# Retention chunks taken two by two between runs of sixteen projection matmuls

## The chip, the cores and the metric

The kernel runs on one core of a Trainium2 chip, as one program. The metric is the device time of one execution in microseconds (us); the median of several executions is compared. The engines that matter here are TensorE (PE: matmuls; its weight loads are listed apart, as PEld), VectorE (DVE) and ScalarE (ACT). Each works through its own instruction list in order, and they wait for one another on semaphores.

## What is computed

Four layers over 1024 tokens of width 1024: a dilated attention layer, a state space layer, and then two "hybrid" layers. Only the retention branch of the hybrid layers is touched. It has 6 heads of 64 channels and works in chunks of 128 tokens, forward and backward in time:

```python
def chunk_retention(q, k, v, lg, s0, inclusive):
    ...
    scores = jnp.einsum('bhnid,bhnjd->bhnij', qc, kc) * dmat[None, :, None]
    o_inner = jnp.einsum('bhnij,bhnje->bhnie', scores, vc)
    ...
    _, s_prev = lax.scan(step, s0, jnp.moveaxis(u, 2, 0))
    ...
    o_cross = jnp.einsum('bhnid,hi,bhnde->bhnie', qc, wq, s_prev)
    return (o_inner + o_cross).reshape(b, h, l, dv)

def bidir_retention(q, k, v, lg_f, lg_b, s_f, s_b):
    fwd = chunk_retention(q, k, v, lg_f, s_f, True)
    bwd = chunk_retention(jnp.flip(q, 2), jnp.flip(k, 2), jnp.flip(v, 2), lg_b, s_b, False)
    return fwd + jnp.flip(bwd, 2)
```

So a chunk needs scores (queries times keys), their product with a decay matrix, the inner output (masked scores times values) and the cross output (queries times the state before the chunk), and both outputs are added. Around it stand the input projections `h @ w_in`, which are by far the larger work.

## The kernel before

Everything is unrolled. A hybrid layer `l` (0 or 1) does its projections in groups `j`, and while PE does the projections of group `hp + 1` it also does the retention of head pair `hp` (0 to 2), whose q, k, v and gate came from group `hp`. In `mix_pe`, `ret_segment(hp)` writes PE's order down by hand: `proj(j, x0, x1)` issues the projection matmuls x0 to x1 of the group, and the retention matmuls are put between such runs at fixed positions (`RET_A` to `RET_F`). 24 projection matmuls make a part; a part is 512 or 256 tokens wide, fills PSUM bank 0 or 1 in turn, and is evacuated by ACT (`evac`), after which that bank may be used again (`g_evac`). A projection matmul is in fp32r, 128 rows by 128 columns of the array.

The chunks: `chunks(l)` is 10 in layer 0 (8 of the sequence, 2 of the context) and 8 in layer 1, so there are 3 x 10 + 3 x 8 = 54. Of one chunk `n` PE issues

- `inner(n)`, the scores: 2 matmuls, one per head, each on 64 rows and 128 columns of the array, into banks 5 and 6 (even n) or 2 and 3 (odd n). It needs those banks read, that is the masked scores of chunk n - 2 (`r_sd`), and for n = 1 the scan of the states (`r_scan`);
- the cross product: 4 matmuls (2 directions x 2 heads) on 64 rows and 64 columns, into bank 7 (even n) or 4 (odd n), once ACT has copied chunk n - 2 out of it (`r_o`);
- the inner output: 2 matmuls on 128 rows and 64 columns, added to the same bank, once DVE has made the masked scores `SD[:, n % 2]` (`r_sd`). The last one releases `r_omul`.

All of these are fp32, and the trace has two MATMUL records for each. DVE makes `SD` of chunk n (L1929) when the scores are there (`r_s`) and, as it has two buffers, when the output of chunk n - 2 is done (`r_omul`). ACT copies the finished chunk to `RO` (L1741) when `r_omul` of that chunk is there, and the evacuations of projection parts stand between these copies on its list. After the last chunk come 10 more projection matmuls and then the matmul that takes the mean (L1554), which waits for all copies.

The constants: `RET_D` = 102 is where `inner(0)` stands, `RET_O` = 112 where the outputs begin, `RET_STEP` = 8. In the loop of before, `proj` runs up to matmul 112 + 8n, then come `inner(n + 1)` and `out_of(n)`, where `out_of` is the cross product and the inner output together.

One other place is spoken of further on: in the state space layer `outputs_of` (L3032, L3041) and `turn_natural` (L822) follow each other on PE, and each begins with a wait (`pe.wait_ge(s_loaded[...], ...)`, `pe.wait_ge(y_gelu, ...)`), though both are work of 128 rows and 128 columns.

Of the kernel before, what the change touches and what calls it, by code (L numbers as in the profile page):

```python
# [133 lines left out]
def build(nc, io, out):  # L134
    x_in = io["x"].rearrange("b s d -> (b s) d")
    ctx = ExitStack()
    with ctx:
# [1167 lines left out]
        def parts_before(l, j):  # L1305
            return sum(len(PARTS[a][b]) for a in range(2) for b in range(N_GROUPS) if (a, b) < (l, j))
# [13 lines left out]
        def n_mms(l, j):  # L1320
            return 24 * len(PARTS[l][j])

        def chunks(l):
            return NC if l == 0 else NT
# [8 lines left out]
        RET_A, RET_B, RET_C, RET_D, RET_O, RET_STEP = 12, 48, 74, 102, 112, 8  # L1333
# [115 lines left out]
        def mix_pe(pe, l, early=None):  # L1449

            def proj(j, x0, x1):

                parts = PARTS[l][j]
                for x in range(x0, min(x1, n_mms(l, j))):
                    i, m = x // 24, x % 24
                    q, c0, c, last = parts[i]
                    n, slot = parts_before(l, j) + i, slot_of(l, j, q)
                    k = m // 3
                    w, a = PASSES[m % 3]
                    if m == 0:  # L1460
                        if j == 0 and q == 0:
                            pe.wait_ge(t_lo, rows_there(l, c0))
                        pe.wait_ge(g_evac[n % 2], EVACS_DONE + n // 2)
                        if c0 == 0:
                            pe.wait_ge(slot_split, slot + 3)
                    ins = nc.tensor.matmul(psum[:, n % 2, 0:c], w[:, slot % 2, k * P:(k + 1) * P], a[:, k, c0:c0 + c],  # L1466
                                           start=(m == 0), stop=(m == 23))
                    if m == 23:
                        ins.then_inc(slot_used if last else half_done, 1)
# [12 lines left out]
            def ret_segment(hp):  # L1482
                j, it = hp + 1, hp + 3 * l
                tk, tv, tq, tg = SETS[hp % 2]
                base = chunk_base(l, hp)

                def inner(n):
                    if n == 1:
                        pe.wait_ge(r_scan, it + 1)
                    if n >= 2:  # L1490
                        pe.wait_ge(r_sd, base + n - 1)
                    for h in range(2):
                        ins = nc.tensor.matmul(psum[:, inner_banks(n)[h], 0:P], tk[HALF[h], n * P:(n + 1) * P],  # L1493
                                               tq[HALF[h], n * P:(n + 1) * P], start=True, stop=True)
                    ins.then_inc(r_s, 1)

                def out_of(n):
                    if n >= 2:
                        pe.wait_ge(r_o, base + n - 1)
                    o = psum[:, cross_bank(n), 0:P]  # L1500
                    for d, v in enumerate((tv, TMP)):
                        for h in range(2):
                            nc.tensor.matmul(o[HALF[h]], SFC[HALF[h], d, n], v[HALF[h], n * P:(n + 1) * P],  # L1503
                                             start=(d == 0), stop=False, skip_group_check=True)
                    pe.wait_ge(r_sd, base + n + 1)
                    for h in range(2):
                        ins = nc.tensor.matmul(psum[HALF[h], cross_bank(n), 0:P], VR[:, n, 64 * h:64 * h + 64],  # L1507
                                               SD[:, n % 2, h * P:(h + 1) * P], start=False, stop=True, skip_group_check=True)
                    ins.then_inc(r_omul, 1)

                proj(j, 0, RET_A)
                group_there(hp)
                if hp == 0:
                    pe.wait_ge(p_const, 16 * 2 * (l + 1))
                if hp > 0:
                    pe.wait_ge(r_eps, it)
                for i, t in enumerate((tk, tq)):
                    for c in range(2):
                        ins = nc.tensor.matmul(psum[:, 2 + 2 * i + c, :], C_PERM, t[:, c * 512:(c + 1) * 512], start=True, stop=True)  # L1519
                    ins.then_inc(r_swap, 1)  # L1520
                for n in range(8):
                    ins = nc.tensor.transpose(psum[:, 6 + n // 4, (n % 4) * P:(n % 4 + 1) * P], tv[:, n * P:(n + 1) * P], ident[:, :])
                    if n % 4 == 3:
                        ins.then_inc(r_vt, 1)
                proj(j, RET_A, RET_B)
                pe.wait_ge(r_rope, 2 * it + 2)
                for n in (8, 9):
                    ins = nc.tensor.transpose(psum[:, 5, (n - 8) * P:(n - 7) * P], tv[:, n * P:(n + 1) * P], ident[:, :])
                ins.then_inc(r_vt, 1)
                for n in range(NC):  # L1530
                    ins = nc.tensor.transpose(psum[:, 2 + n // 4, (n % 4) * P:(n % 4 + 1) * P], tk[:, n * P:(n + 1) * P], ident[:, :])
                ins.then_inc(r_kt, 1)
                proj(j, RET_B, RET_C)
                pe.wait_ge(r_rows, it + 1)
                pe.wait_ge(r_vr, 3 * it + 3)
                for d, w in enumerate((KF, KBW)):
                    for n in range(NC):
                        for h in range(2):
                            ins = nc.tensor.matmul(state_tile(d, n)[HALF[h]], w[:, n, 64 * h:64 * h + 64],  # L1539
                                                   VR[:, n, 64 * h:64 * h + 64], start=True, stop=True)  # L1540
                ins.then_inc(r_u, 1)
                proj(j, RET_C, RET_D)
                inner(0)
                at = RET_D
                for n in range(chunks(l)):
                    proj(j, at, RET_O + RET_STEP * n)
                    at = RET_O + RET_STEP * n
                    if n + 1 < chunks(l):
                        inner(n + 1)
                    out_of(n)  # L1550
                proj(j, at, RET_E[l])
                pe.wait_ge(r_o, base + chunks(l))
                for i, (c0, c) in enumerate(segs_of(l, False)):
                    ins = nc.tensor.matmul(psum[:, 5 + i, 0:c], C_ONES, RO[:, c0:c0 + c], start=True, stop=True)  # L1554
                ins.then_inc(r_mean, 1)
                proj(j, RET_E[l], RET_F[l])
                pe.wait_ge(r_sq, it + 1)
                for i, (c0, c) in enumerate(segs_of(l, False)):
                    ins = nc.tensor.matmul(psum[:, 2 + i, 0:c], C_ONES, TMP[:, c0:c0 + c], start=True, stop=True)
                ins.then_inc(r_var, 1)  # L1560
                proj(j, RET_F[l], n_mms(l, j))
# [76 lines left out]
            for hp in range(3):  # L1638
                ret_segment(hp)
# [3 lines left out]
        def mix_act(act, l, early=False):  # L1643
# [81 lines left out]
            def ret_segment(hp):  # L1725
                j, it = hp + 1, hp + 3 * l
                base = chunk_base(l, hp)
                evacs(j, 0, RET_A)
                for i in range(2):
                    act.wait_ge(r_vt, 3 * it + i + 1)  # L1730
                    C.copy(VR[:, 4 * i:4 * i + 4].rearrange("p n c -> p (n c)"), psum[:, 6 + i, :]).then_inc(r_vr, 1)
                evacs(j, RET_A, RET_B)
                act.wait_ge(r_vt, 3 * it + 3)
                C.copy(VR[:, 8:10].rearrange("p n c -> p (n c)"), psum[:, 5, 0:256]).then_inc(r_vr, 1)
                evacs(j, RET_B, RET_O)
                at = RET_O
                for n in range(chunks(l)):
                    evacs(j, at, RET_O + RET_STEP * n)
                    at = RET_O + RET_STEP * n
                    act.wait_ge(r_omul, base + n + 1)  # L1740
                    C.copy(RO[:, n * P:(n + 1) * P], psum[:, cross_bank(n), 0:P]).then_inc(r_o, 1)  # L1741
                evacs(j, at, RET_E[l])
                if hp < 2:
                    decays(hp + 1)
                w = P * chunks(l)
                act.wait_ge(r_cent, it + 1)
                C.activation(TMP[:, 0:w], RO[:, 0:w], ACT.Square).then_inc(r_sq, 1)
                evacs(j, RET_E[l], RET_F[l])
                act.wait_ge(r_eps, it + 1)
                C.activation(TMP[:, 0:w], TMP[:, 0:w], ACT.Sqrt).then_inc(r_root, 1)  # L1750
                evacs(j, RET_F[l], n_mms(l, j))
# [2102 lines left out]
```

## Time and profile before

| | |
|---|---|
| median of 3 runs | 3284.87 us (3284.24 to 3288.15) |
| profiled execution, its own time | 3281.52 us |
| its span, first to last instruction | 3279.7 us |
| PE busy | 3218.2 us, 98% of the span |
| DVE, ACT, POOL busy | 1409.6, 1242.2, 805.1 us |
| mean granted TensorE clock | 0.998 |
| chunk operations on PE | 54 chunks in 60 places between projection runs |

A row of the timeline gives the start, the time from there to the end of the last instruction of the group, the engine, the line of the kernel and what it does; "64*128" is rows by columns of the array that are used. Matmuls overlap: the time of one is longer than its distance to the next, so the distance between two starts is what an instruction costs PE. The profile's rows are in the section "Rows read from the trace of the kernel before".

### The profile page before, as it was taken

The page shows a single profiled execution, that of the slowest core. Times are in us where ns is not written, and L with a number is a line of the kernel's source. Part 1 is how long each engine was busy: PE and PEld are TensorE (multiplying, and loading weights), DVE is VectorE, ACT ScalarE, POOL GpSimd, SP SyncE. Part 2 cuts the span into 40 slices and gives each one's busy share as a digit, 9 for nine tenths or more (in the row PEclk, how much of TensorE's full clock was granted, in tenths as well). Part 3 has the DMA queues.
Part 4 walks back from the last instruction along what each step waited for, and adds up shares of the span by engine and source line. Part 5 has one row for each costly group of instructions (what it writes and reads, how often), then busy time and mean ns, then how long its engine had stood idle before and what let it go on. Part 6 is the DMA issues. An engine that isn't in the chain of part 4 may idle for free.

```text
span 3279.7 us, 49108 instructions
## 1 busy us (share of the span) xinstructions
PE 3218.2 (98%) x19729; PEld 2572.3 (78%) x19729; DVE 1409.6 (43%) x3279; ACT 1242.2 (38%) x2570; POOL 805.1 (25%) x407
## 2 busy tenths in 40 slices
PE   8999999999999999999999999999999999999999
PEld 6777877788787777778888877777788777777787
DVE  3343223221212137498234344345446724464566
ACT  4443444433443444321323322255333413255342
POOL 2155454111111132324343111101222111110231
PEclk9999999999999999999999999999999999999999
DMA  7122323244434234213534200101104310111113
GB/s 191 44 61 77 84 59 84 66 121 143 110 91 114 79 103 133 93 58 131 206 110 136 65 26 27 33 26 31 30 23 154 98 34 26 31 40 31 33 43 137
DMA packets 311271, 260.99 MB, mean 80 GB/s; under 512 B 61829, under 2 KB 275161, under 8 KB 311050
## 3 DMA queue, kind: packets, MB, share of 16 engines
q10 hardware_dynamic: 115152, 130.49, 13.3%
q1 hardware_dynamic: 195898, 127.41, 13.2%
q8 instruction: 157, 2.57, 0.3%
q14 instruction: 64, 0.52, 0.1%
HBM read 220.87 MB, written 48.58 MB: 82 GB/s over the span
## 4 chain that ended last, share of the span: by engine, by line
PE 53%; DVE 4%; ACT 2%; issue 1%; DMA 1%; ACTq 1%; POOL 0%; DVEq 0%; POOLq 0%
PE psum L1466 24%; PE psum L379 9%; PE psum L301 5%; PE psum L1578 2%; PE psum L1598 2%; PE psum L1587 2%; PE psum L1503 1%; PE psum L3041 1%; DVE act_lo L2472 1%; PE psum L1493 1%; PE psum L1519 1%; PE psum L1507 1%; DVE arena L1908 1%; PE psum L3032 1%; PE psum L1539 0%
## 5 line engine op out<-in xcount | busy, mean ns | idle before, releaser
L2644 POOL TENSOR_TENSOR w_lo<-w_raw,w_hi 128x1024 fp32r<-128x1024 f32 x122 | 294.9, 2417 | 1539.4 <-ACT w_hi L1701 773.2
L1466 PE MATMUL psum<-act_hi,w_hi 128*128 128x512 f32 (+1 forms) x1376 | 513.0, 373 | 4.6 <-ACT arena L1687 2.1
L2814 PE MATMUL psum<-act_hi,w_hi 128*128 128x512 f32 x1280 | 505.4, 395 | 4.7 <-ACT arena L1187 3.6
L2814 PE MATMUL psum<-act_lo,w_hi 128*128 128x512 f32 x1280 | 507.1, 396 | 0.0
L1466 PE MATMUL psum<-act_lo,w_hi 128*128 128x512 f32 (+1 forms) x1376 | 506.8, 368 | 0.0
L1466 PE MATMUL psum<-act_hi,w_lo 128*128 128x512 f32 (+1 forms) x1376 | 505.7, 367 | 0.0
L2814 PE MATMUL psum<-act_hi,w_lo 128*128 128x512 f32 x1280 | 503.4, 393 | 0.0
L3595 DVE CUSTOM_DVE_ANT_0 arena<-psum,arena 128x128 f32<-128x128 f32 (+1 forms) x384 | 112.1, 348 | 480.2 <-PE psum L2853 333.2
L1466 PEld LDWEIGHTS psum<-act_hi,w_hi 128*128 128x128 f32 x1376 | 259.8, 189 | 59.1 <-issue 16.1
L1466 PEld LDWEIGHTS psum<-act_hi,w_lo 128*128 128x128 f32 x1376 | 259.5, 189 | 46.9 <-issue 7.0
L1466 PEld LDWEIGHTS psum<-act_lo,w_hi 128*128 128x128 f32 x1376 | 260.1, 189 | 45.1 <-issue 9.0
L2814 PEld LDWEIGHTS psum<-act_hi,w_hi 128*128 128x128 f32 x1280 | 240.6, 188 | 62.5 <-issue 7.3
L2814 PEld LDWEIGHTS psum<-act_lo,w_hi 128*128 128x128 f32 x1280 | 240.7, 188 | 59.9 <-issue 11.7
L2814 PEld LDWEIGHTS psum<-act_hi,w_lo 128*128 128x128 f32 x1280 | 240.6, 188 | 54.8 <-issue 5.9
L2635 POOL TENSOR_TENSOR w_hi<-w_raw,one 128x1024 fp32r<-128x1024 f32 x48 | 95.1, 1982 | 679.7 <-PE psum L1466 294.7
L1187 ACT ACTIVATE arena<-psum 128x512 f32<-128x512 f32 x144 | 133.0, 923 | 185.6 <-PE psum L2814 155.6
L3131 ACT ACTIVATE arena<-arena 128x128 f32<-128x128 f32 (+1 forms) x384 | 168.5, 441 | 76.6 <-DVE arena L3595 75.9
L3179 ACT COPY arena<-psum 128x1024 f32<-128x1024 f32 (+1 forms) x96 | 83.7, 872 | 269.8 <-PE psum L2871 218.7
L1779 ACT COPY arena<-psum 128x896 f32<-128x896 f32 (+1 forms) x108 | 91.5, 848 | 159.3 <-PE psum L1598 118.2
L2638 POOL TENSOR_TENSOR w_lo<-w_raw,w_hi 128x1024 fp32r<-128x1024 f32 x48 | 125.4, 2613 | 3.8
L1770 ACT ACTIVATE arena<-arena 128x512 f32<-128x512 f32 (+1 forms) x96 | 72.3, 753 | 122.0 <-DVE arena L2003 122.0
L301 PE MATMUL psum<-w_hi,act_hi 128*128 128x512 f32 x256 | 100.2, 391 | 5.8 <-DVE act_lo L452 3.1
(397 smaller groups left out, 5428.6 us busy)
## 6 DMA issues: line engine op xcount, KB each, us to landing
w_raw<-in_attn_w_in SPq DMA_DIRECT2D x80, 512.0 KB, 3.7
w_raw<-in_w_in SPq DMA_DIRECT2D x64, 512.0 KB, 4.0
spare<-in_w_mod ACTq DMA_DIRECT2D x24, 1024.0 KB, 7.9
x<-arena ACTq DMA_DIRECT2D x24, 512.0 KB, 2.9
arena<-weight_rows ACTq DMA_DIRECT2D x16, 512.0 KB, 6.7
w_raw<-in_ssm_w_in SPq DMA_DIRECT2D x16, 512.0 KB, 3.8
arena<-mc_mat ACTq DMA_DIRECT2D x16, 512.0 KB, 3.7
arena<-x ACTq DMA_DIRECT2D x16, 512.0 KB, 5.3
```

The lines of the kernel that those rows point to most:

```text
L301: ins = nc.tensor.matmul(psum[:, t, :], a[:, k, t * P:(t + 1) * P], w[:, par, i * 512:(i + 1) * 512], start=(k == 0 and a is act_hi and w ...
L379: ins = nc.tensor.matmul(psum[:, bank + c, :], a[:, k, t * P:(t + 1) * P], w[:, c * 512:(c + 1) * 512], start=(i == 0 and w is hi and a is ...
L1187: return nc.scalar.activation(dst, src, ACT.Copy, scale=SCALE if p % 3 == 0 else 1.0)
L1466: ins = nc.tensor.matmul(psum[:, n % 2, 0:c], w[:, slot % 2, k * P:(k + 1) * P], a[:, k, c0:c0 + c], start=(m == 0), stop=(m == 23))
L1779: C.copy(PT2[h][:, c0:N_LOG], flat(6, 2)[:, c0:N_LOG]).then_inc(u_pt, 1)
L2635: G.tensor_tensor(w_hi[:, par], w_raw[:, par], one[:, 0:1].to_broadcast([P, 1024]), ALU.mult).then_inc(slot_hi, 1)
L2638: G.tensor_tensor(w_lo[:, par], w_raw[:, par], w_hi[:, par].bitcast(F32), ALU.subtract).then_inc(slot_split, 1)
L2644: G.tensor_tensor(w_lo[:, par], w_raw[:, par], w_hi[:, par].bitcast(F32), ALU.subtract).then_inc(slot_split, 1)
L2814: ins = nc.tensor.matmul(psum[:, h % 2, :], w[:, (3 + j) % 2, k * P:(k + 1) * P], a[:, k, c:c + 512], start=(m == 0), stop=(m == 23))
L3131: nc.scalar.activation(lg, lg, ACT.Exp, scale=-1.0, bias=st[:, 2 + h, u:u + 1], accum_out=st[:, h, u:u + 1]).then_inc(u_probs, 1)
L3179: nc.scalar.copy(PT.rearrange("p a (h c) -> p a h c", h=2)[:, :, :, 0:c], psum[:, 4:6, :].rearrange("p a (h c) -> p a h c", h=2)[:, :, :, ...
L3595: nc.vector.tensor_tensor_reduce(LOG[:, a, h * 256:h * 256 + P * nk], psum[:, 2 + h, 256 * a:256 * a + P * nk], BIAS[:, h, bias_cols(g, u) ...
```

## The change

The cross product becomes a function of its own, `cross(n)`. The chunks are taken in pairs: after a run of projection matmuls come the scores of chunks n + 2 and n + 3, the cross products of n and n + 1, and then the inner outputs of n and n + 1. The runs between pairs are 16 matmuls instead of 8. `inner(1)` stands alone at position 112, and the first pair comes at 120. On ACT the copies of both chunks of a pair stand at the pair's position in its list. DVE's list is the same. Positions of all later work (`RET_E`, `RET_F`) are unchanged.

```diff
@@ -1494,7 +1494,7 @@
-                def out_of(n):
+                def cross(n):
                     if n >= 2:
                         pe.wait_ge(r_o, base + n - 1)
                     o = psum[:, cross_bank(n), 0:P]
@@ -1502,6 +1502,8 @@
                         for h in range(2):
                             nc.tensor.matmul(o[HALF[h]], SFC[HALF[h], d, n], v[HALF[h], n * P:(n + 1) * P],
                                              start=(d == 0), stop=False, skip_group_check=True)
+
+                def out_of(n):
                     pe.wait_ge(r_sd, base + n + 1)
                     for h in range(2):
                         ins = nc.tensor.matmul(psum[HALF[h], cross_bank(n), 0:P], VR[:, n, 64 * h:64 * h + 64],
@@ -1541,13 +1543,19 @@
                 inner(0)
-                at = RET_D
-                for n in range(chunks(l)):
-                    proj(j, at, RET_O + RET_STEP * n)
-                    at = RET_O + RET_STEP * n
-                    if n + 1 < chunks(l):
-                        inner(n + 1)
+                proj(j, RET_D, RET_O)
+                inner(1)
+                at = RET_O
+                for n in range(0, chunks(l), 2):
+                    proj(j, at, RET_O + RET_STEP * (n + 1))
+                    at = RET_O + RET_STEP * (n + 1)
+                    if n + 2 < chunks(l):
+                        inner(n + 2)
+                        inner(n + 3)
+                    cross(n)
+                    cross(n + 1)
                     out_of(n)
+                    out_of(n + 1)
                 proj(j, at, RET_E[l])
@@ -1735,8 +1743,8 @@
                 for n in range(chunks(l)):
-                    evacs(j, at, RET_O + RET_STEP * n)
-                    at = RET_O + RET_STEP * n
+                    evacs(j, at, RET_O + RET_STEP * (n // 2 * 2 + 1))
+                    at = RET_O + RET_STEP * (n // 2 * 2 + 1)
                     act.wait_ge(r_omul, base + n + 1)
                     C.copy(RO[:, n * P:(n + 1) * P], psum[:, cross_bank(n), 0:P]).then_inc(r_o, 1)
```

PE's list, layer 0, first head pair, before: the places of chunks 1 and 2, with the run of 8 projection matmuls between them cut. In these rows 128x128 and 64x128 are the shapes of the output. L1493 are scores, L1503 cross products, L1507 inner outputs.

```order
L1493 MATMUL psum<-arena 128x128 [waits r_sd]
L1493 MATMUL psum<-arena 128x128
L1503 MATMUL psum<-arena 64x128 x4
L1507 MATMUL psum<-arena 64x128 [waits r_sd]
L1507 MATMUL psum<-arena 64x128
L1466 MATMUL psum<-act_hi,w_hi 128x256 [waits g_evac1]
...
L1493 MATMUL psum<-arena 128x128 [waits r_sd]
L1493 MATMUL psum<-arena 128x128
L1503 MATMUL psum<-arena 64x128 [waits r_o]
L1503 MATMUL psum<-arena 64x128 x3
L1507 MATMUL psum<-arena 64x128 [waits r_sd]
L1507 MATMUL psum<-arena 64x128
```

The same place now: the pair of chunks 2 and 3 (scores of 4 and 5), where L1509 are the inner outputs.

```order
L1493 MATMUL psum<-arena 128x128 [waits r_sd]
L1493 MATMUL psum<-arena 128x128
L1493 MATMUL psum<-arena 128x128 [waits r_sd]
L1493 MATMUL psum<-arena 128x128
L1503 MATMUL psum<-arena 64x128 [waits r_o]
L1503 MATMUL psum<-arena 64x128 x3
L1503 MATMUL psum<-arena 64x128 [waits r_o]
L1503 MATMUL psum<-arena 64x128 x3
L1509 MATMUL psum<-arena 64x128 [waits r_sd]
L1509 MATMUL psum<-arena 64x128
L1509 MATMUL psum<-arena 64x128 [waits r_sd]
L1509 MATMUL psum<-arena 64x128
```

Operations of one kind and one shape of the array now stand in a row for two chunks, and the second of each kind has a wait in the middle of that row.

ACT's list, the same layer and head pair, before (L1689 evacuates a projection part, L1701 rounds weights, L1741 copies a chunk):

```order
L1689 COPY arena<-psum 128x512 [waits half_done]
L1741 COPY arena<-psum 128x128 [waits r_omul]
L1689 COPY arena<-psum 128x512 [waits half_done]
L1741 COPY arena<-psum 128x128 [waits r_omul] x3
L1689 COPY arena<-psum 128x256 [waits slot_used]
L1701 CAST w_hi<-w_raw 128x1024 [waits slot_hi,slot_loaded1]
L1741 COPY arena<-psum 128x128 [waits r_omul] x3
```

And now (L1697, L1709 and L1749 are the same three):

```order
L1697 COPY arena<-psum 128x512 [waits half_done] x2
L1749 COPY arena<-psum 128x128 [waits r_omul] x4
L1697 COPY arena<-psum 128x256 [waits slot_used]
L1709 CAST w_hi<-w_raw 128x1024 [waits slot_hi,slot_loaded1]
L1749 COPY arena<-psum 128x128 [waits r_omul] x2
```

The copies moved behind the evacuation of the part that ends at the first pair, and the later ones come two by two.

## Rows read from the trace of the kernel before

**Rows 1.** The page: busy time of the engines, and the chain by engine.

```profile
PE 3218.2 (98%) x19729; PEld 2572.3 (78%) x19729; DVE 1409.6 (43%) x3279; ACT 1242.2 (38%) x2570; POOL 805.1 (25%) x407
...
PE 53%; DVE 4%; ACT 2%; issue 1%; DMA 1%; ACTq 1%; POOL 0%; DVEq 0%; POOLq 0%
```

**Rows 2.** Windows: one head pair, layer 0: PE, PEld, DVE, ACT, POOL busy; clock.

```profile
1860.00:1944.00 84.00, 83.91 (x570) 64.36 (x569) 35.07 (x52) 22.24 (x43) 9.82 (x4) 1.00 0.09 26
```

**Rows 3.** Waits of weight loads, 1800 to 3182 us: total us, times, longest.

```profile
PEld psum L1493 <- issue: 15.9, 45, 0.4
...
PEld psum L1507 <- DVE arena L1929: 8.3, 48, 0.2
```

**Rows 4.** Timeline of PE: one place of before, between 512-wide projection matmuls.

```profile
1892.41 0.39 PE L1466 MATMUL psum<-act_hi,w_hi 128*128 128x512 f32 x1
1892.73 0.49 PE L1493 MATMUL psum<-arena 64*128 64x128 f32 x4
1893.15 0.65 PE L1503 MATMUL psum<-arena 64*64 64x128 f32 x8
1893.74 0.44 PE L1507 MATMUL psum<-arena 128*64 128x128 f32 x4
1894.11 0.50 PE L1466 MATMUL psum<-act_lo,w_hi 128*128 128x512 f32 x1
1894.44 0.39 PE L1466 MATMUL psum<-act_hi,w_lo 128*128 128x512 f32 x1
1894.67 0.40 PE L1466 MATMUL psum<-act_hi,w_hi 128*128 128x512 f32 x1
```

**Rows 5.** Timeline of PE: another place, between 256-wide projection matmuls.

```profile
1898.34 0.28 PE L1466 MATMUL psum<-act_hi,w_hi 128*128 128x256 f32 x1
1898.46 0.28 PE L1466 MATMUL psum<-act_lo,w_hi 128*128 128x256 f32 x1
1898.67 0.49 PE L1493 MATMUL psum<-arena 64*128 64x128 f32 x4
```

**Rows 6.** One line: DVE's masked scores, all 54 (duration min/median/max).

```profile
L1929 DVE TENSOR_TENSOR arena<-psum,arena x54: 424/425/426, 1890.4 to 2853.8; 128x256 f32<-128x256 f32 x54
```

**Rows 7.** Timeline of PE in the attention layer: four matmuls on 64*128 in a row.

```profile
70.97 0.72 PE L2827 MATMUL psum<-arena 64*128 64x128 f32 x8
71.61 0.50 PE L2814 MATMUL psum<-act_hi,w_hi 128*128 128x512 f32 x1
```

**Rows 8.** Timeline of PE in the neighbourhood attention: twelve matmuls on 128*64 in a row.

```profile
2154.45 1.53 PE L1598 MATMUL psum<-arena 128*64 128x128 f32 x24
2155.91 0.70 PE L1578 MATMUL psum<-arena 64*128 64x512 f32 x2
```

**Rows 9.** Timeline of PE in the state space layer: groups of equal shape, each behind a wait.

```profile
1580.19 0.60 PE L822 MATMUL psum<-ident,arena 128*128 128x128 f32 x4
1580.63 0.61 PE L3032 MATMUL psum<-arena 128*128 128x128 f32 x4
```

**Rows 10.** Timeline of DVE: masked scores of the chunk whose scores stand in rows 4.

```profile
1893.27 0.42 DVE L1929 TENSOR_TENSOR arena<-psum,arena 128x256 f32<-128x256 f32 x1 [2.49 <-PE psum L1493]
```

**Rows 11.** Timeline of ACT: copy of the chunk of rows 4, and a later part.

```profile
1894.22 0.27 ACT L1741 COPY arena<-psum 128x128 f32<-128x128 f32 x1 [5.07 <-PE psum L1507]
...
1903.80 0.37 ACT L1689 COPY arena<-psum 128x256 f32<-128x256 f32 x1 [0.87 <-PE psum L1466]
1904.07 1.05 ACT L1701 CAST w_hi<-w_raw 128x1024 fp32r<-128x1024 f32 x1
```

**Rows 12.** Timeline of PE: the end of the last chunk of layer 1, to the mean.

```profile
2857.68 0.38 PE L1466 MATMUL psum<-act_hi,w_hi 128*128 128x256 f32 x1
...
2858.97 0.59 PE L1554 MATMUL psum<-arena 128*128 128x512 f32 x1
```

**Rows 13.** Timeline of ACT there: the part before that chunk, and the chunk's copy.

```profile
2856.83 0.59 ACT L1693 COPY arena<-psum 128x512 f32<-128x512 f32 x1 [1.76 <-PE psum L1466]
2857.79 0.27 ACT L1741 COPY arena<-psum 128x128 f32<-128x128 f32 x1 [0.38 <-PE psum L1507]
```

## Prediction

> **What bounds the kernel now.** I read the page first. PE is busy 98% of the span, and the chain that ended last is mostly PE, while DVE, ACT and POOL are busy 43, 38 and 25% [rows 1]. Then the windows: in the 84 us around the retention of one head pair PE is busy 83.91 us at a granted clock of 1.00 (2.4 GHz), while DVE has 35 and ACT 22 us of work [rows 2]. Whatever shortens PE's list there shortens the program, as long as nothing else gets late.
>
> Next, what PE does in those 84 us. A busy row does not say that PE works at its peak, so I read starts. The waits list puts 8.3 us in 48 pieces of at most 0.2 us on "DVE L1929", and 15.9 us in 45 pieces of at most 0.4 us on "issue" [rows 3]. Neither is a true wait: DVE had finished the masked scores of that chunk a step earlier, and pieces of one size at each change of line look like a fixed price. The timeline shows it [rows 4]. Projection matmuls start 0.23 us apart (1894.44 to 1894.67). Around a chunk the starts are 1892.41 (last projection), 1892.73 (scores), 1893.15 (cross), 1893.74 (inner output), 1894.11 and 1894.44 (projections). From this a place costs:
>
> - entry: 1892.73 - 1892.41 - 0.23 = 0.09
> - scores I (4 records): 1893.15 - 1892.73 = 0.42
> - cross X (8 records): 1893.74 - 1893.15 = 0.59
> - inner output O (4 records): 1894.11 - 1893.74 = 0.37
> - exit: 1894.44 - 1894.11 - 0.23 = 0.10
>
> Together 1.57 us. Between 256-wide matmuls, 0.12 apart, the entry is the same: 1898.67 - 1898.46 - 0.12 = 0.09 [rows 5].
>
> Each kind uses another shape of the array (128*128, 64*128, 64*64, 128*64). How much of I, X and O is the price of changing shape and how much is streaming follows from longer runs of one shape. Four matmuls on 64*128 (8 records) take 71.61 - 70.97 = 0.64 us to the next shape [rows 7], where two take 0.42 [rows 4]. Twelve matmuls on 128*64 (24 records) take 2155.91 - 2154.45 = 1.46 us [rows 8], where two (4 records) take 0.37 [rows 4]: the other 20 records cost 1.09, or 0.055 each.
>
> **The change, part by part.** It removes no matmul and adds none. It changes how often PE changes shape.
>
> *Places.* Before, one head pair had `inner(0)`, and then one place per chunk: 11 in layer 0 and 9 in layer 1, times three, 60. Now there are `inner(0)`, `inner(1)` and one place for two chunks: 7 and 6, times three, 39. So 21 entries and exits go: 21 x 0.19 = 4.0 us.
>
> *Scores.* Two chunks' scores stand in a row 4 times per head pair in layer 0 and 3 times in layer 1, 21 in all. Two single I cost 0.84, a double one 0.64 [rows 4, 7]: 21 x 0.20 = 4.2 us.
>
> *Inner outputs.* Doubled 5 and 4 times, 27 in all. The second adds 4 x 0.055 = 0.22 instead of 0.37: 27 x 0.15 = 4.05 us.
>
> *Cross products.* Doubled 27 times. No row shows a longer run on 64*64. The bounds are that nothing is saved (the second costs 0.59 again) and that as much is saved as in the scores (0.20). I take 0.055 for each of the 8 records of the second, the pace of the 128*64 run, which moves the same 128 columns per record and has two matmuls side by side too: 0.44 instead of 0.59, 27 x 0.15 = 4.05 us (0 to 5.4).
>
> The sum is 4.0 + 4.2 + 4.05 + 4.05 = 16.3 us (12.3 to 17.7 by the bounds of the cross product).
>
> *The added waits inside a row* (the second scores, the second cross product, the second inner output: 21 + 21 + 27 = 69) I cost at nothing, if the semaphore is there in time. In the state space layer the group of L3032 also has a wait of its own and has the same shape as that of L822 ahead of it: 1580.63 - 1580.19 = 0.44 for 4 records, 0.11 each, no break [rows 9].
>
> *Are they in time?* DVE first, the cover that changes most. It makes `SD` of chunk n + 2 when the output of n is done. Before, that was past when the scores arrived, so DVE began 0.12 after them (1893.15, 1893.27), with a whole run in hand [rows 4, 10]. Now both products of a pair begin only when `out_of(n)` and `out_of(n + 1)` are done, at the end of the place. Two products of 0.425 us [rows 6] and some 0.12 us of signal for each make about 1.1 us, and the next scores, which wait for the first of them, come after 16 projections: 16 x 0.12 = 1.9 us in the one run that is 256 wide throughout, up to 16 x 0.23 = 3.7 in the others. Slack 0.8 us and more. The first pair's `inner(3)` waits for `SD` of chunk 1, whose scores stand 8 wide projections, 1.8 us, ahead, and the product ends 0.12 + 0.42 = 0.54 us after the scores: in time. Nothing else is queued on DVE there but the next head pair's decays, behind the last product, which now come 8 projections earlier.
>
> ACT: copies of 0.27 us, now two after each place, needed by the cross products 16 projections later. Between them stand evacuations (0.59 or 0.37 us) and a rounding of weights (1.05 us) [rows 11, 13]. Where a part ends just at a place, this work begins with the place, and a double place lasts 0.64 + 1.03 + 0.59 = 2.3 us, so ACT is free (0.59 + 1.05 = 1.6 us) when the place ends. At the end of a layer 1 pair the mean comes 1.29 us after the place (2857.68 to 2858.97) [rows 12]; the last copy now starts when the one before it ends, some 0.1 us later than before, when it ended 0.38 us after the place (2857.79 + 0.27 = 2858.06) [rows 13]. Slack 0.8 us. POOL and SP have the same lists, and their weights are needed at the same positions, 3 us in 84 earlier, with POOL busy 10 us of 84 [rows 2].
>
> *A rule against it.* In the run of rows 8 the matmuls of one pair and the next use the same rows of the array, and a pair of records costs 0.11 us, no more than the streaming, so their weight loads lie under the matmuls in flight. The Trainium skill, "TensorE: Matmul & The Clock Gate", part 3 (packing small matmuls), states that a weight load overlaps matmuls in flight only when its row group differs; by that rule the loads in the doubled rows would stay exposed, which is rival 2 below. Rows 8 speak against it.
>
> The profiled execution took 3281.52 us for a span of 3279.7, and the median is 3284.87, 3.3 us more; I take the gain off the median: 3284.87 - 16.3 = **3268.6 us** (a profiled execution at about 3265).
>
> **The rivals.**
>
> 1. *A wait in a row costs as much as a change of shape.* Then 21 double scores, 21 double cross products and 27 double outputs save nothing: 4.2 + 3.15 + 4.05 = 11.4 us less gain, 4.9 us left, 3280.0 us. For it: the waiting loads in the list are all at changes of shape, so this pattern is not in the retention. Against: rows 9. Chance 3%.
>
> 2. *Weight loads of the second chunk stay exposed.* A first load shows in the starts as 0.42 - 2 x 0.11 - 0.10 (the entry's size, for draining) = 0.10 us on 128 columns, and 0.37 - 2 x 0.11 - 0.10 = 0.05 on 64 [rows 4]. The second scores have two such steps (0.20), the second cross four (0.20), the second output two (0.10). The savings become 0, -0.05 and 0.05: 0 - 1.35 + 1.35 + 4.0 = 4.0 us, 3280.9 us. Against: rows 7 and 8. Chance 3%.
>
> 3. *Slower: the products of DVE get late.* They are tied to the end of a place, and PE waits for them at the next. The point from which it costs anything is a chain of 1.9 us (3.7 in wide runs) against my 1.1. To end slower by 6.6 us it must eat 16.3 + 6.6 = 22.9 us in the 21 places that begin with scores, 1.1 us each, so a chain of some 4.8 us in wide runs. For it: it is the one dependence that really became tighter. Against: 54 products of 424 to 426 ns without exception [rows 6]. Chance 2% for slower; 4% for a few places that wait, 3270 to 3277 us.
>
> 4. *The order doesn't reach the hardware.* It does: the list has the rows two by two. What may still go is the gain after it, if a later stage waits for something that does not follow PE. The chain has 1% of DMA [rows 1]; 3% that over 9.7 us is lost there and the result is within 0.2%.
>
> **How the numbers follow.** Forecast 85%, rivals 3, 3, 2 (and 4 for its mild form) and 3. The forecast's own range is 12.3 to 17.7 us of gain, 3267 to 3273, and the runs of before spread from 0.6 below to 3.3 above their median. I take 3264 to 3276: it holds the forecast and most of the mild form. A measurement of this kernel can tell about 0.2%, 6.6 us, from no change, so faster is below 3278.3: 85 + 4 + 1 = 90%; rivals 1, 2 and most of 4 are the same: 8%; slower 2%.
>
> **What would show it.** In the profile of the changed kernel, a full place should have its scores (8 records) 0.64 us ahead of the cross products, these (16 records) 1.03 us ahead of the inner outputs, and these (8 records) 0.59 us ahead of the projection; entry 0.09 and exit 0.10. 2.45 us stand for two places of 1.57. The "L1929" wait should fall from 48 pieces to one per place, 27 (24 with scores, fewer where it is named otherwise), still at most 0.2 us. If the cross takes 1.18, the upper bound was right; if the second of a kind starts 0.1 us late, rival 1 or 2, told apart by whether it is at the waiting record alone or at every pair. A longer idle row with L1929 behind it ahead of L1493 is rival 3. What would make the forecast wrong with all of this right is a wait on DMA or POOL that grew elsewhere by 10 us.

## The result

| | before | after |
|---|---|---|
| median | 3286.36 us (5 runs, 3284.24 to 3288.15) | 3268.76 us (5 runs, 3263.08 to 3275.58) |
| ratio after / before | | 0.9948, 95% interval 0.9935 to 0.9962 |
| profiled execution, span | 3279.7 us, clock 0.998 | 3273.8 us, clock 0.993 |
| places on PE | 60, 86.0 us | 39, 69.7 us |

The forecast was 3268.6 us. Five more executions of the changed kernel, taken later, gave 3268.93 (first experiment below).

The page of the changed kernel, the same rows as [rows 1]:

```profile
PE 3211.9 (98%) x19729; PEld 2579.8 (79%) x19729; DVE 1405.6 (43%) x3279; ACT 1241.6 (38%) x2570; POOL 800.1 (24%) x407
...
PE 53%; DVE 4%; ACT 2%; issue 1%; DMA 1%; ACTq 1%; POOL 0%; DVEq 0%; POOLq 0%
```

PE has the same number of records and is still the engine that is busy all the time; nothing took its place. What changed is seen in its timeline. The first double place (columns as in [rows 4]):

```profile
1906.01 0.39 PE L1466 MATMUL psum<-act_lo,w_hi 128*128 128x512 f32 x1
1906.23 0.39 PE L1466 MATMUL psum<-act_hi,w_lo 128*128 128x512 f32 x1
1906.55 0.71 PE L1493 MATMUL psum<-arena 64*128 64x128 f32 x8
1907.20 1.09 PE L1503 MATMUL psum<-arena 64*64 64x128 f32 x16
1908.22 0.66 PE L1509 MATMUL psum<-arena 128*64 128x128 f32 x8
1908.80 0.38 PE L1466 MATMUL psum<-act_hi,w_hi 128*128 128x256 f32 x1
1909.03 0.28 PE L1466 MATMUL psum<-act_lo,w_hi 128*128 128x256 f32 x1
```

Scores 0.65 us, cross products 1.02, inner outputs 0.58, entry 1906.55 - 1906.23 - 0.23 = 0.09, exit 1909.03 - 1908.80 - 0.12 = 0.11: 2.45 us, where two places of [rows 4] took 2 x 1.57. With 12 single scores of 0.62 us, 21 places of 2.45 and 6 last ones of 1.80 the sum is 69.7 us; before it was 6 x 0.62 + 48 x 1.57 + 6 x 1.15 = 86.0. That is 16.3 us less.

**The profiled execution is an odd one.** Its span is only 5.9 us shorter, not 16.3. The starts of `inner(0)` tell where the rest went. First the kernel before, then the one after: head pairs 0 and 1 of layer 0, and 0 and 1 of layer 1.

```profile
1889.82 0.38 PE L1493 MATMUL psum<-arena 64*128 64x128 f32 x2
1973.85 0.38 PE L1493 MATMUL psum<-arena 64*128 64x128 f32 x2
2681.41 0.38 PE L1493 MATMUL psum<-arena 64*128 64x128 f32 x2
2755.67 0.38 PE L1493 MATMUL psum<-arena 64*128 64x128 f32 x2
```

```profile
1901.18 0.38 PE L1493 MATMUL psum<-arena 64*128 64x128 f32 x2
1982.11 0.38 PE L1493 MATMUL psum<-arena 64*128 64x128 f32 x2
2682.71 0.38 PE L1493 MATMUL psum<-arena 64*128 64x128 f32 x2
2754.57 0.38 PE L1493 MATMUL psum<-arena 64*128 64x128 f32 x2
```

A head pair of layer 0 takes 80.93 us in place of 84.03, one of layer 1 71.86 in place of 74.26. The gain per head pair is 3.10 and 2.40 us. But the first scores of the first head pair are reached 11.36 us later than in the profile of before. Most of that happened in the stretch shown here (windows: PE, PEld, DVE, ACT, POOL busy, granted clock, DMA share, GB/s), before and after:

```profile
1200.00:1300.00 100.00, 90.15 (x552) 71.51 (x549) 60.90 (x103) 48.51 (x88) 40.97 (x16) 1.00 0.46 138
1300.00:1400.00 100.00, 93.59 (x535) 76.28 (x534) 45.59 (x74) 38.21 (x76) 26.96 (x12) 1.00 0.28 93
```

```profile
1200.00:1300.00 100.00, 89.97 (x504) 70.70 (x503) 50.48 (x88) 44.39 (x77) 35.50 (x15) 0.90 0.40 116
1300.00:1400.00 100.00, 95.54 (x478) 78.09 (x476) 46.27 (x80) 40.42 (x82) 26.96 (x12) 0.97 0.29 97
```

The granted clock fell there, to 0.90 and 0.97 in the mean of 100 us, so PE did 504 matmul records where it had done 552 in the first of these windows. In the next 100 us it was 0.98. Together 10 + 3 + 2 = 15 us of full clock are missing by 1500 us, of which 11.36 came out as delay; PE was busy 90 to 96% of that time. It is work that stands ahead of every changed instruction and is the same in both kernels.

### The profile page after: what moved, and what is told of

Its sections match the earlier page's. It is cut to its first block, busy times and chain, and to the rows that moved or that the text cites. A ratio compares the mean times of both kernels' runs of the same rounds, so it can differ in the third digit from the quotient of the medians.

```text
span 3273.8 us, 49108 instructions
## 1 busy us (share of the span) xinstructions
PE 3211.9 (98%) x19729; PEld 2579.8 (79%) x19729; DVE 1405.6 (43%) x3279; ACT 1241.6 (38%) x2570; POOL 800.1 (24%) x407
## 4 chain that ended last, share of the span: by engine, by line
PE 53%; DVE 4%; ACT 2%; issue 1%; DMA 1%; ACTq 1%; POOL 0%; DVEq 0%; POOLq 0%
PE psum L1466 24%; PE psum L379 9%; PE psum L301 5%; PE psum L1586 2%; PE psum L1606 2%; PE psum L1595 2%; PE psum L3049 1%; PE psum L1503 1%; DVE act_lo L2480 1%; PE psum L1521 1%; DVE arena L1916 1%; PE psum L1493 1%; PE psum L3040 1%; PE psum L1509 0%; PE psum L3024 0%
```

## The experiments

**More executions.** The changed kernel, unchanged.

> The changed kernel again, unchanged, for more executions with their clocks. Theory (the time follows the places on TensorE, 86.06 us of them before and 69.69 now, and the rest of the spread is the granted clock): 3264 to 3271 us, 16 us (0.5%) under the kernel before in the median, and executions with a mean granted clock of 0.998 lie near 3263 to 3267, those with 0.993 some 10 us above. Rival (the change itself brings the lower clock): the clock of this kernel is below 0.998 in most executions while that of the kernel before stays at 0.998.

Measured: 3268.93 us (3260.25 to 3269.99, 5 runs), before 3286.14 (3281.65 to 3290.22, 20 runs) on the same chip, ratio 0.9945 (0.9931 to 0.9959). Clocks of the changed kernel 0.996 to 0.999, of the kernel before 0.995 to 0.998, and on another chip two of the 11 executions of the kernel before had 0.994 and 0.993 and took 3290.63 and 3297.89 us. So the lower clock comes to both kernels; the change doesn't bring it. The clock orders the times only roughly: 0.999 goes with 3260.25, but 0.998 with 3268.93, 2 us above what I had expected.

**Which part carries the gain: places or shapes.** Two kernels keep the 39 places and undo the order inside. In the first, the scores stay doubled:

```diff
-                    cross(n)
-                    cross(n + 1)
-                    out_of(n)
-                    out_of(n + 1)
+                    for m in (n, n + 1):
+                        cross(m)
+                        out_of(m)
```

> From the changed kernel: the scores stay doubled and the places stay 39, but cross product and inner output alternate chunk by chunk (X O X O in place of X X O O). Theory (each change of the array's shape costs about 0.10 us of draining and the exposed first weight load): a double place takes 0.645 + 2 x 0.953 + 0.197 = 2.75 us in place of 2.45 and a last one 2.10 in place of 1.81, so 27 x 0.30 = 8.1 us of the 16.4 are given back: 3277 us, ratio to before 0.9975. Rival (the gain is in having fewer places between the projections, not in the shapes inside): a place stays at 2.45 us and the time at 3269.

Measured: 3276.95 us (10 runs), ratio 0.9974 (0.9965 to 0.9984). The first double place, PE's timeline:

```profile
1900.13 0.39 PE L1466 MATMUL psum<-act_hi,w_lo 128*128 128x512 f32 x1
1900.45 0.72 PE L1493 MATMUL psum<-arena 64*128 64x128 f32 x8
1901.09 0.65 PE L1503 MATMUL psum<-arena 64*64 64x128 f32 x8
1901.68 0.44 PE L1509 MATMUL psum<-arena 128*64 128x128 f32 x4
1902.05 0.65 PE L1503 MATMUL psum<-arena 64*64 64x128 f32 x8
1902.63 0.44 PE L1509 MATMUL psum<-arena 128*64 128x128 f32 x4
1903.00 0.39 PE L1466 MATMUL psum<-act_hi,w_hi 128*128 128x256 f32 x1
1903.22 0.28 PE L1466 MATMUL psum<-act_lo,w_hi 128*128 128x256 f32 x1
```

Cross product and output take 0.59 and 0.37 us again, as in [rows 4], the second time too, although no projection stands between them. The place has 2.75 us.

In the second, the scores alternate as well:

```diff
-                    if n + 2 < chunks(l):
-                        inner(n + 2)
-                        inner(n + 3)
-                    cross(n)
-                    cross(n + 1)
-                    out_of(n)
-                    out_of(n + 1)
+                    for m in (n, n + 1):
+                        if n + 2 < chunks(l):
+                            inner(m + 2)
+                        cross(m)
+                        out_of(m)
```

> From the changed kernel: the 39 places stay, but inside each the two chunks follow one another as in the kernel before (scores, cross, output, then scores, cross, output). Theory: only 21 entries and exits of 0.197 us remain as a gain, 4.1 us: a double place takes 2 x 1.375 + 0.197 = 2.95 us, the time is about 3282 us, ratio 0.9988. Rival (fewer places carry the gain): 3269 us and 2.45 us a place.

Measured: 3281.22 us (11 runs), ratio 0.9988 (0.9979 to 0.9997). Its first double place starts at 1897.03 and the projection behind it at 1899.78, 2.75 us, 2.95 with entry and exit:

```profile
1897.03 0.49 PE L1493 MATMUL psum<-arena 64*128 64x128 f32 x4
...
1898.41 0.49 PE L1493 MATMUL psum<-arena 64*128 64x128 f32 x4
...
1899.78 0.39 PE L1466 MATMUL psum<-act_hi,w_hi 128*128 128x256 f32 x1
```

Both came out on the theory's numbers (3277 and 3282). By the lengths of the places, fewer places alone are worth 4 us, doubled scores another 4, doubled cross products and outputs the remaining 8; by the medians it is 4.9, 4.3 and 8.0 us. The rival, that only the number of places counts, is out: it gave 3269 for both. That the shape of the array counts and not merely the step from one line of the kernel to another follows from [rows 9], where the line changes, the shape does not, and there is no break.

**A wait in the middle of a row.** This is rival 1 of the prediction, made 150 times: in the scores from the third chunk of a head pair on (3 x 8 + 3 x 6 = 42), and in all 54 cross products and 54 inner outputs. The 156 of the expectation is a miscount.

```diff
                     for h in range(2):
+                        if n >= 2 and h == 1:
+                            pe.wait_ge(r_scan, it + 1)
                         ins = nc.tensor.matmul(psum[:, inner_banks(n)[h], 0:P], ...
...
                     for d, v in enumerate((tv, TMP)):
+                        if d == 1:
+                            pe.wait_ge(r_scan, it + 1)
...
                     for h in range(2):
+                        if h == 1:
+                            pe.wait_ge(r_scan, it + 1)
                         ins = nc.tensor.matmul(psum[HALF[h], cross_bank(n), 0:P], ...
```

> From the changed kernel: a wait more in the middle of every operation (ahead of the second matmul of scores and inner output, and ahead of the second direction of the cross product), on a semaphore that has long been reached (r_scan): 156 added waits inside rows of one shape. Theory (a wait that is satisfied costs TensorE nothing inside a row): places stay at 2.45 and 1.81 us, 69.7 us in all, and the time at 3269. Rival 1 of the prediction (a wait breaks the row like a change of shape): 156 x 0.10 to 0.20 = 16 to 31 us more, 3285 to 3300.

Measured: 3269.65 us (4 runs), ratio 0.9946 (0.993 to 0.9963), and the same place as in the changed kernel:

```profile
1900.18 0.72 PE L1495 MATMUL psum<-arena 64*128 64x128 f32 x8
1900.83 1.09 PE L1507 MATMUL psum<-arena 64*64 64x128 f32 x16
1901.85 0.66 PE L1515 MATMUL psum<-arena 128*64 128x128 f32 x8
1902.44 0.38 PE L1466 MATMUL psum<-act_hi,w_hi 128*128 128x256 f32 x1
```

0.65, 1.02 and 0.59 us, and all 39 places take 69.7 us in both kernels. Here a wait that is satisfied costs nothing in a row of one shape.

**How far VectorE is from being late.** This is rival 3. Each masked product is made three times, two of them into space that is not used at that time:

```diff
                     b = inner_banks(n)[0]
+                    for k in range(2):
+                        V.tensor_tensor(region(512 + 256 * (2 * k + n % 2), 2, P), psum[:, b:b + 2, 0:P], DM[:, :, :], ALU.mult)
                     V.tensor_tensor(SD[:, n % 2].rearrange("p (h c) -> p h c", h=2),
                                     psum[:, b:b + 2, 0:P], DM[:, :, :], ALU.mult).then_inc(r_sd, 1)
```

> From the changed kernel: VectorE makes each masked product three times (two into unused space, the third as before). Two real products take 0.76 us after a place, from 0.04 us ahead of its end; six take about 0.42 + 5 x 0.36 = 2.2 us. The next scores come 2.1 us after the place in the narrow run (layer 0, second pair) and their second half 0.3 us later. Theory (slack of 1.37 us in the narrow run, more elsewhere): at most 0.1 us of wait in three places, none elsewhere; places in all 69.7 to 70.3 us. Rival (the slack is smaller than it looks, semaphores are slow): 0.3 us or more in each of the 21 places with scores, 6 us and more.

Measured, one execution: 3267.09 us, and every place as long as in the changed kernel, 69.7 us in all. The spare products hide altogether, and the rival is out.

Then six times, `range(5)` in the same edit. The spare products of this one reach into a finished part of the branch's result, so only its time is read.

> From the changed kernel: each masked product six times. Twelve products take 0.42 + 11 x 0.36 = 4.4 us after a place. The second scores of the next place, which wait for them, come 2.4 us after the place in the narrow run, 3.3 in the mixed one and 4.2 in the wide ones. Theory: waits of 2.0 to 2.2, 1.1 to 1.3 and 0.1 to 0.5 us: per head pair some 3.5 us in layer 0 and 0.6 in layer 1, 12 us in all (8 to 17), 3281 us. This is rival 3 of the prediction made true by force; the kernel would end slower than before only with a chain longer than this. Rival (TensorE is hardly tied to VectorE here): 3269 us.

Measured: 3276.95 us (8 runs), ratio 0.9969 (0.9955 to 0.9983), 8.0 us more than the changed kernel of the first experiment; the places sum to 78.2 us, 8.5 more. PE in the narrow run of the second head pair, and DVE ahead of it:

```profile
1988.35 0.49 PE L1493 MATMUL psum<-arena 64*128 64x128 f32 x4
1990.33 0.49 PE L1493 MATMUL psum<-arena 64*128 64x128 f32 x4 [1.50 <-DVE arena L1939]
```

```profile
1986.21 1.75 DVE L1938 TENSOR_TENSOR arena<-psum,arena 128x256 f32<-128x256 f32 x5 [2.06 <-PE psum L1509]
1987.88 0.41 DVE L1939 TENSOR_TENSOR arena<-psum,arena 128x256 f32<-128x256 f32 x1
1988.21 1.74 DVE L1938 TENSOR_TENSOR arena<-psum,arena 128x256 f32<-128x256 f32 x5
1989.87 0.41 DVE L1939 TENSOR_TENSOR arena<-psum,arena 128x256 f32<-128x256 f32 x1
```

The second scores wait for the second product, 1.50 us, and the place takes 4.21 us. The places that waited were those of the narrow run of layer 0 (1.8 us more) and, in the second and third head pair, of its mixed run (0.9 us more); the wide runs had 0.02 and none. The mechanism is the one of the theory, the size is at its lower end: 8 us where 12 (8 to 17) was expected. The term that was off is the distance of products in a row, 0.33 us in these rows (1986.21 to 1987.88 for five) and not the 0.36 that I took: over eleven of them that is 0.33 us, about what each wait fell short of the expected one.

In one of these places, in the first head pair, the wait was followed by more. Windows around it:

```profile
1899.50:1903.80 4.30, 4.30 (x49) 3.75 (x48) 2.23 (x8) 1.07 (x3) 0.00 (x0) 1.00 0.02 4
1903.80:1906.20 2.40, 0.91 (x10) 0.60 (x8) 2.01 (x7) 0.00 (x0) 0.00 (x0) 1.00 0.00 0
1906.20:1909.60 3.40, 3.40 (x30) 2.65 (x27) 0.82 (x3) 0.53 (x2) 0.00 (x0) 0.55 0.00 0
```

PE had been idle for 1.5 of 2.4 us, and in the next window the granted clock was 0.55, nearly all of it at 1.2 GHz. The place took 5.50 us in place of 4.21. The other two waits of the same length were not followed by that: the granted clock stayed at 1.00. What decides it stays open.

**Further along the same way.** If the price is for changes of shape, fours must beat pairs. The kernel puts the scores of four chunks at position 112 and then has places at 128, 160 and 184 (layer 0) or 136 and 168 (layer 1), with four buffers of masked scores and two chunks in one PSUM bank (the edit is shown against the kernel before, in extracts):

```diff
-        SD = region(0, 2, 256)
+        SD = region(0, 4, 256)
...
+        FOURS = (((0, 4, 128), (4, 8, 160), (8, 10, 184)), ((0, 4, 136), (4, 8, 168)))
...
-                    if n >= 2:
-                        pe.wait_ge(r_sd, base + n - 1)
+                    if n >= 4 and n % 4 == 0:
+                        pe.wait_ge(r_sd, base + n)
...
-                                             start=(d == 0), stop=False, skip_group_check=True)
+                                             start=(d == 0 and n % 4 < 2), stop=False, skip_group_check=True)
...
+                for n0, n1, x in FOURS[l]:
+                    proj(j, at, x)
+                    at = x
+                    for n in range(n0 + 4, min(n1 + 4, chunks(l))):
+                        inner(n)
+                    for n in range(n0, n1):
+                        cross(n)
+                    for n in range(n0, n1):
+                        out_of(n)
...
-                    act.wait_ge(r_omul, base + n + 1)
+                    act.wait_ge(r_omul, base + min(n // 4 * 4 + 4, chunks(l)))
```

Two chunks share a bank, so the second one's first matmul carries no `start`. The Trainium skill, "PSUM — Partial Sum Buffer", section "The four PSUM rules", states that `start` (`first_mm` there) clears the accumulate marks of the whole bank in the quadrants of 32 partitions that the output touches, so that two groups open at once in the same bank and quadrant can't both use it; no run here shows what happens otherwise. As the banks are shared, ScalarE and VectorE also wait for the whole group of four before they read.

> From the changed kernel: chunks four by four. Scores of four chunks stand alone at position 112, then places at 128, 160 and 184 (layer 0) or 136 and 168 (layer 1), with four buffers for the masked scores and two chunks in one PSUM bank; waits on a bank go by the whole group of four. Theory: the price of shapes is paid 21 times in place of 39 and all runs of one shape are twice as long: per head pair 1.29 + 4.20 + 3.76 + 1.80 = 11.05 us in place of 12.84 (layer 0) and 1.29 + 4.20 + 3.11 = 8.60 in place of 10.39 (layer 1), 10.7 us in all: 3258 us, ratio 0.992. Rival (a new wait: ScalarE copies four chunks only after a place ends, 4 x 0.27 + 0.11 = 1.2 us, against 1.29 us to the mean in layer 1, and VectorE needs some 2 us for four products): a wait ahead of the mean or ahead of the next scores, which gives back up to 1 us a place, 3258 to 3275.

Measured: 3258.9 us (3255.51 to 3259.44, 5 runs), ratio 0.9918 (0.9904 to 0.9931). Against the changed kernel on the same chip (3260.25 to 3269.99) it is 10.0 us faster, and its places sum to 59.0 us in place of 69.7. A place of four, PE's timeline:

```profile
1900.26 1.16 PE L1498 MATMUL psum<-arena 64*128 64x128 f32 x16
1901.35 1.96 PE L1508 MATMUL psum<-arena 64*64 64x128 f32 x32
1903.25 1.09 PE L1514 MATMUL psum<-arena 128*64 128x128 f32 x16
1904.27 0.38 PE L1471 MATMUL psum<-act_hi,w_lo 128*128 128x256 f32 x1
```

1.09, 1.90 and 1.02 us. The feared wait ahead of the mean of layer 1 is not there: ScalarE's four copies end 2835.34 + 0.77 = 2836.11, and the mean starts at 2836.51, so 0.40 us are left.

```profile
2835.34 0.77 ACT L1752 COPY arena<-psum 128x128 f32<-128x128 f32 x4 [2.34 <-PE psum L1514]
2836.51 1.88 PE L1565 MATMUL psum<-arena 128*128 128x512 f32 x4
```

## Why the prediction was right

The mechanism is the one of the forecast, and its four terms came out one by one. That the time agrees to 0.2 us is luck: executions of the changed kernel spread over 15 us, and the median of before, off which I took the gain, was 3284.87 us in three executions and 3286.36 in five, so the measured gain is 17.6 us where I had 16.3. The profiled execution, which I put at about 3265 us, took 3275.58, for the clock's reason given above.

*The bound.* PE's list set the time, and 16.3 us less in its places gave 17.6 and 17.2 us less in the medians, within their intervals (12.5 to 21.4 us by the first). No later stage gave the gain back: the waits of PE behind the changed segments are those of before to 0.2 us (5.6, 2.1, 2.0 and 1.2 us where it was 5.8, 2.1, 2.1 and 1.2), and in the profiled execution the later start of 11.36 us and the gain of 3 x (3.10 + 2.40) = 16.5 us in the head pairs make 5.1 of the 5.9 us less of span.

*Places*, 21 x 0.19 = 4.0 us. The kernel in which nothing but the number of places changed was 4.1 us faster by its places and 4.9 us in the medians, ratio 0.9988 (0.9979 to 0.9997).

*Scores*, 21 x 0.20. A double one takes 0.65 us, as L2827 does in [rows 7].

*Inner outputs*, 27 x 0.15. A double one takes 0.58 or 0.59 us, as worked out from [rows 8].

*Cross products*, 27 x 0.15, with bounds of 0 and 5.4 us since no row showed a longer run. The second adds 1.02 - 0.59 = 0.43 us, so the pace of the 128*64 run was the right row to take (0.44). In fours the step is the same: (1.90 - 1.02) / 2 = 0.44.

With rows for one, two and four chunks each kind lies on a line: scores 0.42, 0.65, 1.09 us, cross products 0.59, 1.02, 1.90, inner outputs 0.37, 0.58, 1.02. A chunk adds 0.22, 0.44 and 0.22 us, and what is left, 0.20, 0.15 and 0.15 us, is paid once per row however long it is. The row of twelve matmuls in [rows 8], as many as six chunks have, fits: 0.15 + 6 x 0.22 = 1.47 us for 1.46. With entry and exit that makes about 0.70 us per place: 0.70 + 0.88 n gives 1.58, 2.46 and 4.22 us for n = 1, 2 and 4, and the traces have 1.57, 2.45 and 4.21.

*Waits in a row at nothing*: shown, with 150 more of them. Rival 1 is out. *Weight loads hidden* within a row: every further pair of records costs 0.11 us in rows of up to 32. Rival 2 would have made a double row of scores 0.84 us and one of outputs 0.69; they take 0.65 and 0.58. The rule of the Trainium skill ("TensorE: Matmul & The Clock Gate", part 3) that a load overlaps only where the row group differs doesn't hold for these matmuls: the outputs use all 128 rows, and their loads are hidden. (The same part of the Trainium skill also lets a load for the background weight buffer be pulled ahead of matmuls in flight; no run here tells whether that is the way.)

What is shown is the price of a change as a whole. How it divides into draining (about 0.10 us, the size of entry and exit) and a first weight load that nothing hides (0.05 to 0.10 us) is my working from the starts, and no experiment separates the two. That there is a draining part agrees with the Trainium skill, "TensorEngine Tiling (Array Packing)", "Key Properties", which says that switching the tiling mode drains TensorE; it gives no time for it.

*DVE in time*: right, with a chain shorter than I had reckoned. In the changed kernel, behind the place shown above and ahead of scores at 1910.90:

```profile
1908.77 0.76 DVE L1937 TENSOR_TENSOR arena<-psum,arena 128x256 f32<-128x256 f32 x2 [3.72 <-PE psum L1509]
1910.90 0.71 PE L1493 MATMUL psum<-arena 64*128 64x128 f32 x8
```

The products of both chunks end at 1909.53, 0.73 us after the place (1908.80) and not 1.1: in a row they start 0.33 us apart, though each lasts 0.42, and the first begins before the projection. The slack in the narrowest run is 1910.90 - 1909.53 = 1.37 us, not 0.8. The chain with three products of each had no effect and the one with six had, in narrow and mixed runs only.

*ACT in time*: right, and here too I was too careful. The last copies of a layer 1 pair end 2851.70 + 0.48 = 2852.18, 0.38 us after the place (2851.80), just as in [rows 12, 13].

```profile
2851.70 0.48 ACT L1749 COPY arena<-psum 128x128 f32<-128x128 f32 x2 [0.81 <-PE psum L1509]
2851.80 0.39 PE L1466 MATMUL psum<-act_hi,w_hi 128*128 128x256 f32 x1
```

*What I said the profile would show*: the lengths came as written. The wait named after DVE's line is gone altogether; one piece per place, 27 of 0.17 us each, is there, but under "issue". Before, the pieces had the same size (8.3 us in 48), so they had never been a wait for DVE. (The "24 with scores" in that passage is a slip: 21 of the 27 begin with scores, as the terms above it have it.)

```profile
PEld psum L1493 <- issue: 10.6, 30, 0.4
...
PEld psum L1509 <- issue: 4.6, 27, 0.2
```

*The range*: the spread between executions, 3260 to 3276 us for the same kernel, is as large as the gain. It goes, roughly, with the mean granted clock, and in the profiled execution the low clock lay outside the changed segments (1.00 from 1860 to 2120 and from 2650 to 2870 us), so a single pair of executions could have shown nothing. The profiled one nearly did (6 us).

## What to carry to other kernels

Small matmuls woven between large ones pay for each change of the array's shape, here about 0.70 us for the four changes of a place, whatever the number of chunks in it; group them by shape over as many independent pieces as buffers allow, and count changes of shape, not instructions. Read the price from the distance between starts, since the busy share shows 98% with or without it. A wait that was sure to be satisfied stood in such a group at no cost, but the consumers' deadlines become tighter with each doubling, and the slack is read from where the other engine ends and where PE asks.

## What the runs showed of the hardware that I had not expected

- DVE products of 128 x 256 that last 0.42 us each start 0.33 us apart in a row, and ACT copies of 0.27 us make 0.48 us for two and 0.77 for four. A sum of single durations overstates these chains: by a tenth for two products or two copies (0.84 for 0.76, 0.54 for 0.48) and by two fifths for four copies (1.08 for 0.77).
- The granted clock of one and the same kernel was 0.993 to 0.999 in the mean from execution to execution, with some 15 us in the time: the changed kernel took 3260.25 us at 0.999 and 3275.58 at 0.993, the kernel before 3281.65 at 0.998 and 3297.89 at 0.993. In the profile of the changed kernel the falls lay at 1200 to 1500 us, where PE has short waits, at 2500 to 2700 us (0.98) and in the last 273 us (0.99); in that of the kernel before only at 2500 to 2700 us (0.98). Why an execution has more or fewer of them stays open.
